# Nine gather buffers instead of twelve, and three expert query weights loaded before the gathers

## The reference

```python
def peer_ffn(h, w_q, sub_keys, u, v):      # 256 tokens in two blocks of 128, D = 1024
    q = (xb @ w_q).reshape(n, 8, 2, 128)                 # 8 heads, a query in two halves
    s = jnp.einsum('nhpc,hpkc->nhpk', q, sub_keys)       # each half against 128 keys
    s_top, i_top = lax.top_k(s, 16)
    cand_s = s_top[:, :, 0, :, None] + s_top[:, :, 1, None, :]    # 16 x 16 pairs
    best_s, best_pos = lax.top_k(cand_s, 16)
    ids = jnp.take_along_axis(cand_i, best_pos, axis=-1)          # 16 experts of 16384
    gate = jax.nn.softmax(best_s, axis=-1)
    act = gelu(jnp.einsum('nd,nhkd->nhk', xb, u[ids]))
    return jnp.einsum('nhk,nhkd->nd', gate * act, v[ids])
...
x = x + merged @ w_o[l]
x = x + peer_ffn(rms_norm_2(x, g_ffn[l]), ...)
return rms_norm_2(x, g_final)
```

## Time and profile before

| | us |
|---|---|
| median of 3 runs | 2027.92 (2026.99 to 2028.90) |
| the profiled execution | 2027.99 |
| its span, first to last instruction | 2026.2 |
| PE busy | 1866.7 (92% of the span) |
| DVE busy | 1056.6 (52%) |
| ACT busy | 505.3 (25%) |
| POOL busy | 323.8 (16%) |
| first gather issued | 1357.0 |
| last gather issued | 1996.3 |

### The profile page before, as it was taken

One profiled execution on the slowest core, in us unless ns is written; L12 is line 12 of the kernel. 1 busy time (PEld: TensorE's weight loads), 2 busy tenths in 40 slices (PEclk: granted clock), 3 DMA queues, 4 the chain that ended last, 5 costly groups with the idle time before them and its releaser, 6 DMA issues.

```text
span 2026.2 us, 20909 instructions
## 1 busy us (share of the span) xinstructions
PE 1866.7 (92%) x8020; PEld 1381.0 (68%) x8020; DVE 1056.6 (52%) x2575; ACT 505.3 (25%) x1226; POOL 323.8 (16%) x341
## 2 busy tenths in 40 slices
PE   6999999999999999999999999998888887887777
PEld 5877788888887788888888787885343342443332
DVE  6996665401797422001201432236867677767755
ACT  2043221111214222110012545121322222222223
POOL 1000001000000000000000000013443444444441
PEclk9999999999999999999999999999999999998999
DMA  9614469844352143449552323529999999999996
GB/s 397 262 55 159 186 253 422 343 157 150 134 209 81 64 182 134 159 153 208 218 199 99 116 101 117 216 110 422 421 421 421 421 421 421 421 421 422 420 421 277
DMA packets 72435, 517.39 MB, mean 255 GB/s; under 512 B 8208, under 2 KB 8464, under 8 KB 11664
## 3 DMA queue, kind: packets, MB, share of 16 engines
q0 software_dynamic: 46384, 330.85, 40.7%
q1 hardware_dynamic: 25952, 185.21, 24.1%
HBM read 510.78 MB, written 5.24 MB: 255 GB/s over the span
## 4 chain that ended last, share of the span: by engine, by line
PE 57%; DMA 20%; DVE 18%; ACT 3%; issue 1%; POOL 1%; DVEq 0%; SPq 0%; POOLq 0%; ACTq 0%
DMA region<-in_peer_uv,small 18%; PE pj L624 12%; PE pj L887 10%; PE pj L902 9%; DVE region L1713 9%; PE st L1170 6%; PE pj L830 5%; DVE region L2125 2%; PE pj L637 2%; PE pj L931 1%; PE pj L1141 1%; DMA ring<-in_ring_w 1%; PE st L1089 1%; PE ms L830 1%; PE pj L922 1%
## 5 line engine op out<-in xcount | busy, mean ns | idle before, releaser
L1170 PE MATMUL st<-region 128*128 128x512 f32 x940 | 453.3, 631 | 111.5 <-ACT region L1549 111.5
L1170 PEld LDWEIGHTS st<-region 128*128 128x128 f32 x940 | 182.3, 200 | 361.7 <-issue 189.3
L624 PE MATMUL pj<-hT,ring 128*128 128x256 f32 x1760 | 385.0, 380 | 1.0 <-ACT region L1353 1.0
L2125 DVE CUSTOM_DVE_ANT_0 region<-region 128x1024 f32<-128x1024 f32 x235 | 287.3, 1224 | 163.7 <-DMA region<-in_peer_uv,small 161.3
L624 PEld LDWEIGHTS pj<-hT,ring 128*128 128x128 f32 x1760 | 332.6, 190 | 47.1 <-ACT region L1353 1.8
L528 POOL DMA_INDIRECT region<-in_peer_uv,small x235 | 259.4, 1104 | 393.6 <-PE st L1170 322.4
L887 PE MATMUL pj<-region,ring 128*128 128x256 f32 x1024 | 222.0, 379 | 0.5 <-DMA ring<-in_ring_w 0.5
L887 PEld LDWEIGHTS pj<-region,ring 128*128 128x128 f32 x1024 | 194.3, 190 | 28.0 <-DMA ring<-in_ring_w 0.9
L1549 ACT ACTIVATE region<-ident,small 128x128 f32<-128x128 f32 x256 | 89.2, 394 | 456.1 <-DVE small L2133 456.1
L1713 DVE SCALAR_TENSOR_TENSOR region<-region,pc 128x255 f32<-128x255 f32 (+19 forms) x528 | 202.6, 462 | 0.0
L1664 DVE TENSOR_TENSOR tmp<-xT,hT 128x256 f32<-128x256 f32 x32 | 13.6, 425 | 359.1 <-ACT hT L1249 359.1
(11 more groups left out here) (382 smaller groups left out, 1987.0 us busy)
## 6 DMA issues: line engine op xcount, KB each, us to landing
ring<-in_ring_w SPq DMA_DIRECT2D x157, 1024.0 KB, 4.8
region<-in_ada_rest POOLq DMA_DIRECT2D x40, 1024.0 KB, 12.4
region<-in_ada_first SPq DMA_DIRECT2D x8, 1024.0 KB, 18.6
region<-in_wqkv SPq DMA_DIRECT2D x2, 3072.0 KB, 12.1
region<-in_wcmp POOLq DMA_DIRECT2D x2, 2048.0 KB, 9.9
bias_dram<-region POOLq DMA_DIRECT2D x1, 4096.0 KB, 46.0
region<-in_w_o POOLq DMA_DIRECT2D x4, 1024.0 KB, 7.1
region<-in_peer_uv,small POOLq DMA_INDIRECT x235, 17.0
```

The costliest lines, as they stand in the source:

```text
L624: i = nc.tensor.matmul(b[:, m, :], w[:, k, P * m:P * m + P], hT[:, k, :], start=(k == 0), stop=(k == CT - 1))
L1170: i = nc.tensor.matmul(acc[:, u % 2, 512 * hf:512 * hf + 512], diag[:, m % NDIAG, :], uv[m % NBUF][:, D + 512 * hf:D + 512 * hf + 512], st ...
L2125: nc.vector.tensor_tensor_reduce(row, row, h_tok[:, u % 2, :], 1.0, 0.0, ALU.mult, ALU.add, dots[:, u, k:k + 1]).then_inc(sem("u_used"), 1)
```

## The change

`NBUF` goes from 12 to 9, and `FREE` from 6 to 3. The three buffers given up hold the weights of heads 5, 6 and 7, which POOL loads from `ring_w` after `w_o[3]`, once `o_kept` is 10. SP leaves these three out. PE takes them from there and waits for `mem_in`, which all three raise, at 64. `LATE` names the heads and places. Nothing else differs: the order of work on PE, DVE and ACT, the ring and `LAG` are the same. Row n now waits for row n - 9. Rows 0 to 2 wait for nothing but the numbers, rows 3 to 6 for `acc_made`, row 7 for `query0_made`, row 8 for `sums_open`.

```diff
-NBUF = 12
+NBUF = 9
+LATE = {5: 16384, 6: 18432, 7: 22528}
...
-        uv = [piece(lo, 2 * D) for lo in (4096, 6144, 14336, 16384, 18432, 22528, 12288, 20480, 24576, 10240, 26624)]
+        uv = [piece(lo, 2 * D) for lo in (4096, 6144, 14336, 12288, 20480, 24576, 10240, 26624)]
         uv += [xT[:, :, :].rearrange("p c t -> p (c t)")]
-        FREE = 6
+        FREE = 3
+        late_query = {f"peer_q{j}": piece(lo, SLOT) for j, lo in LATE.items()}
...
             for n, (name, l, j) in enumerate(jobs):
-                if n >= RING:
+                if n >= RING and name not in late_query:
...
             pool.dma_start(w_o[3], a["w_o"][3].rearrange("p (k n) -> p k n", k=CT)).then_inc(sem("w_o_in"), 16)
+            pool.wait_ge(sem("o_kept"), len(UNITS))
+            for name, dst in late_query.items():
+                pool.dma_start(dst, a["ring_w"][job_at[(name, 2, 0)]]).then_inc(sem("mem_in"), 16)
...
             def second_slot(name):
+                if name in late_query:
+                    pe.wait_ge(sem("mem_in"), 16 + 16 * len(late_query))
+                    return late_query[name]
                 return ring_slot((name, 2, 0))
```

## The result

| | before | after |
|---|---|---|
| median, us | 2028.11 (20 runs) | 2033.12 (20 runs) |
| lowest run | 2026.61 | 2028.75 |
| profiled execution | 2027.99 | 2037.03 |
| its span | 2026.2 | 2035.3 |

The ratio is 1.0023, with a 95% interval of 1.0016 to 1.0030: 5.0 us slower at the medians. That is inside the range (2026.0 to 2035.5), but 4.2 us above the forecast of 2028.9 and above the forecast's own range, which ended at 2032.5. One run of the change, 2761.94 us at a granted clock of 0.654 where the others have 0.98 to 0.99, was disturbed; without it the median is 2032.92, 4.8 us above before. One thing stands out before any trace is read: the runs of before lie within 3 us, those of the change spread from 2028.75 to 2037.03. The profiled execution is the slowest of them, so it shows what is lost, and more of it than the median does.

A forecast was written before the change was run, and what follows sets the result against it. The prediction took the stage of the rows to be bound by DMA transfers, after a start where compute is behind. A late start, +3.4 us, less one regained load, 2.5, gave +0.9 on 2027.99: 2028.9 us, range 2026.0 to 2035.5.

The forecast's parts named there:

- the balance it spoke of: Stage of the rows: a late start, +3.4 us, against one regained load, -2.5 us; chance 0.75.
- the slower rival: After the start, the queue runs dry once per head because nine buffers leave too little reserve; 2040.4 us, chance 0.17.
- The forecast itself, +0.9: Whole kernel: 2028.9 us against the profiled 2027.99, own range 2027.0 to 2032.5, chance 0.75.
- the prediction's own signs: Changed profile: DMA gaps only between about rows 12 and 27; a busy share below full after 1450 us means the slower rival.
- Each takes 2.49 us of a DMA that has no free time, so the gross worth is 7.5 us: Stage of the rows: the loads `peer_q5`, `peer_q6` and `peer_q7` leave the saturated DMA, 7.5 us gross.
- The three loads ahead of row 0 cost nothing: POOL, from about 1312 us: the three added loads fit before the first row at 1357.0; cost nothing.
- The early waits of the first rows cost nothing: Rows 3, 7 and 8: waits come three rows earlier, rows 7 and 8 some 2 us later behind 17 us of queue; no cost.
- The DMA is 3.4 us late: Start, row 27: issued at 1435.0, lands after 5.7 us at 1440.7 instead of 1437.3, and the delay stays.
- So there nine buffers suffice, barely. Cost there: nothing: Rows after the start: shortest flights of 13.7 to 15.1 us all exceed the needed 13.2, so no loss.
- The subtraction from the earlier trace: With nine buffers, a row's flight is that of the row three later before, less three landings, 7.5 us.
- Only the third load counts: -2.5: `peer_q5` and `peer_q6` move before row 27 and gain nothing; only `peer_q7`, in the full stretch, gains 2.5 us.
- The time to landing from the Trainium skill's page: Row 27 at the start: a 4.4 us flight makes it 2.1 us late, sum -0.4 us, 2027.6; the prediction preferred 5.7.

The follow-up runs named there:

- one load and the gain: Twelve buffers, head 7's weight and the final gain loaded before row 0 into freed score and query columns, against the kernel before: 2024.46 us, ratio 0.9981.
- The start alone: Twelve buffers and ring loads as before, only rows 9 to 39 wait as if there were nine, against the kernel before: 2031.07 us, ratio 1.0015.
- Ten in flight: Twelve buffers and ring loads as before, rows from 48 on wait as if there were ten, against the kernel before: 2027.96 us, ratio 1.0000.
- the one comparison on one chip: Nine buffers with all ring loads, 2038.71 us, beside nine buffers with only head 7's weight loaded ahead, 2037.49 us.
- the best version: Eleven buffers, weights of heads 6 and 7 and the final gain loaded ahead, freed score and query columns used, against the kernel before: 2022.08 us, ratio 0.9976.

## Why the prediction was right, and where it was not

The range held the time, and the balance it spoke of was the right kind: the loads' gain against a queue that became too short. But the range held it because it took in half of the slower rival. The forecast itself, +0.9, had a range of its own up to 2032.5, and 2033.1 lies above that. By the prediction's own signs, too, a share below full after 1450 us (0.99 from 1600 to 1700) meant the slower rival. That rival, given 0.17, is what came, at a lower price than it named. Its single steps:

- **"Each takes 2.49 us of a DMA that has no free time, so the gross worth is 7.5 us": right.** Without the loads and with all buffers, -7.0 us; for one load, -3.0; for one load and the gain, -3.9.
- **The three loads ahead of row 0 cost nothing: right.** They landed by 1322.0 us, and row 0 was issued at 1357.7; the seven traces without late loads have it between 1357.0 and 1357.9, so the shift from 1357.0 is not theirs.
- **The early waits of the first rows cost nothing: right.** Rows 7 and 8 came 2.1 and 3.1 us later with a full queue ahead.
- **"The DMA is 3.4 us late" from the start: right in size, by luck.** The start alone cost 2.9 us in the median. But row 27 took 9.0 us and not 5.7, and was 6.2 us late in that kernel's trace; with all ring loads and nine buffers it took 7.6 and was 2.7 late. That the median came so near is two errors that pull against each other: the flight into a dry queue was taken too short, and compute was later in the trace of before than it is in most executions.
- **"So there nine buffers suffice, barely. Cost there: nothing": this step failed.** It cost 2.1 us alone, with a shortest flight of 6.3 us and a median of 9.9, as worked out. The subtraction from the earlier trace rows was right; the yardstick was not. The 5.7 us of row 0 is the time of one row with nothing around it, not the time that keeps 16 engines busy: row 85 was late with 8.2. Ten in flight lost nothing that can be seen. The slower rival named this mechanism and its condition (more than 6.2 us needed), and took the 8.5 us of row 1 for it, which gives too much: 8.7 us against 2.1. It charged the lowest row of each stretch in full, where the trace shows the two lowest rows on time. The Trainium skill's page "Perfetto Trace Analysis", section "Optimization Strategy", says that repeated gaps can mean too few buffers. The trace of the change agrees, with the reservation that the profile's share line stands at nines and only the GB/s, 400 to 421, show them.
- **"Only the third load counts: -2.5": not confirmed.** By the parts, 2.9 + 2.1 - 2.5 is +2.5, and the change measured +5.0 and +5.5. At nine buffers, moving this load brought 1.2 us by medians and 3.0 by means in the one comparison on one chip, which neither shows the 2.5 nor excludes it. Whether the gap is the lost load or nine buffers' own spread from chip to chip (5.8 and 10.9 us for one kernel) is open. That the start swallows a moved load fits ten buffers, where 5.0 us of loads brought 0.9, but no run parts the load from the two buffers there.
- **The time to landing from the Trainium skill's page "DMA: Bandwidth & Descriptors", section "Anatomy of one DMA — SWDGE (gpsimd) path"** (4.4 us for a row, an estimate by its fit) would have put the change at -0.4 us. The lone row 0 took 5.7 us, and the measured +5.0 decides against using the page's time, or any time of a lone transfer, as the depth that a full queue needs.

## What to carry to other kernels

When a stage is bound by transfers, bytes taken out of it count in full and buffers count for nothing, until the shortest time in flight comes near the limit. So look at the minimum of the time to landing, subtract what each buffer is worth (one transfer's time), and stop well above the time of a lone transfer, here at one buffer of twelve and not at three. To see whether a queue has run low, read GB/s and not the busy share; to see what it costs, compare when the same rows land, since the mean of 16 engines overstates it. And before giving up a buffer, look for a place that holds more than is alive: two heads' scores instead of eight made room for a weight at no cost, and the best version, 2022.1 us, uses both.

## What the runs showed of the hardware that was not expected

- The DMA busy share stayed at 0.99 to 1.01 while the rate fell from 421 to between 402 and 414 GB/s. In the short queue a packet takes longer, and the longer time counts as busy: by share and rate a packet of 8 KB took about 314 ns before (1.01 at 421) and 323 after (0.99 at 402), an estimate that takes every packet as 8 KB.
- The 16 engines don't finish together. In the kernel before, the last 5 us before the last row landed moved 25 GB/s at a share of 0.06, one engine of 16. So when a row lands goes by the last engine and not by the mean.
- A row of 1 MB took 5.7 us into an empty queue, but 8.2 and 8.6 us in the nearly dry queue of the changed kernel, and 9.0 us for row 27 with the short queue at the start alone.
- Kernels at this edge vary from run to run by up to 8 us, where the kernel before varies by 2 to 3.3 (but for one run of 94, 3 us above the others) and the one with eleven buffers and one moved load by 1.4. The best version, eleven buffers and more taken out, varies by 5.6. One and the same kernel, nine buffers with all ring loads, lost 5.8 us on one chip and 10.9 on another. A kernel that is short of transfers in flight is also one whose measurement says less.
